# Hybrid transformer layer: the pool branch product computed between projections and attention, the values projected as rows

## The chip, the cores and the metric

The kernel runs on one core of a Trainium2 chip. The metric is the device time of one execution in microseconds, the median of several runs. The engines named below are PE (TensorE, the matmuls), ACT (ScalarE), DVE (VectorE), POOL (GpSimd) and SP, whose queue here only issues DMAs. All data is fp32; a matmul that needs full precision is made of three passes over operands split into a high part (rounded, "hi") and a low part (the rest, "lo"): hi times hi, hi times lo, lo times hi.

## What is computed

One layer for 256 context tokens and 1024 latent tokens, 1280 in all, of width 1024. Cut to what matters here:

```
h = RMSNorm(x) * (1 + scale1) + shift1
q, k, v, xp, ga, gb = split(h @ w_in)            # 1024, 256, 256, 512, 1024, 1024 columns
q, k = rope(RMSNorm(q)), rope(RMSNorm(k))        # 8 query heads, 2 key/value heads of 128
attn = softmax(q k^T / sqrt(128)) v              # latent queries: 1024 latent + 512 cached keys; context queries: 256 context keys
pool = multiscale_pool(xp, w_pool) * pool_scale  # 512 channels
merged = sigmoid(ga) * (attn @ w_branch_a) + sigmoid(gb) * (pool @ w_branch_b)
x = x + gate1 * (merged @ w_out)
# then a second norm, the router, 16 experts and the final norm; k and v of the context tokens are outputs too
```

## The kernel before

Activations are held transposed: 128 channels on the partitions, the 1280 tokens along the free axis, in column groups of 512, 512 and 256 (`GROUPS`). Each engine has its own hand-written instruction list per block; semaphores alone tie them together, and every engine works strictly in the order of its list.

**Block 1, projections.** `project(n, j)` (L311) makes 128 output channels: 8 slices k of 128 input channels, for each the three hi/lo passes over the three column groups, 72 matmuls, into the PSUM half `par_sets[j]`. ACT casts each weight half to `w_hi[j]` once the previous product that used the buffer is finished (`split`, L448), POOL subtracts to get `w_lo[j]` (L539). The pairs come in the order pool input, gates, q, k (`K0` = 14), v (`V0` = 15). The norm and rope of head j of a pair hang on the next product: `sums` (sums of squares by a matmul with ones, L387) as a hook after its slice 2, `spread` (the reciprocal roots to all partitions, L396) after slice 5; between them ACT takes the root and DVE refines it; after them ACT copies the spread rows out, DVE scales the product (L715, frees the PSUM half), makes the sine part (L722), POOL the cosine part (L557), DVE adds (L725). For keys, ACT then casts to `kT_hi` (L518) and POOL makes `kT_lo` (L560). POOL's list in this place reads: w_lo of v half 0, cosine of key head 0, w_lo of v half 1, cosine of key head 1, kT_lo of both heads. The values are projected like everything else (`project(V0, 0)`, `project(V0, 1)`), copied out by ACT (L525), turned into rows by 20 PE transposes (L417), and copied into `vals` by ACT (L530) and DVE (L744). At the end POOL makes the low part of the cached keys (L562). The pool branch's 512 channels go to memory as `poolT`, the sigmoids of the 16 gate rows as `gates`. The block ends in a barrier, the clearing of its semaphores (L749) and a second barrier.

**Block 2, attention.** 16 latent units (one key/value head, 128 tokens, 4 query heads each) and 4 short context units run through `over_units` (L815). `head` makes the scores of one query head (9 matmuls of 512 columns, L875 to L877; DVE finds the maxima, L1022; ACT takes the exponential, L946), `block_` turns the probabilities (L901) and multiplies by values (L885). In front of the steady loop stands an opening of five steps g, in which the four query heads of unit 0 and the four short units are worked side by side: on PE `head(g)`, `short_turn(g-1)` (L926), `short_score(g)` (12 matmuls of 256 columns, L915 to L917), `short_value(g-1)` (L934), the last step with head 0 of unit 1. A short unit's scores go to DVE (maximum L1040, scaled L1041), ACT (four exponentials L965), DVE (normalised, L1047), PE (turned), ACT and DVE (copied out, L970, L1051), PE (values). ACT's and DVE's lists hold the same steps in the same order. POOL splits q (L987, L990) and clears `stage` (L1011) first of all; SP fills the 12 tiles of `y_sum` from it.

**Block 3, merge.** For each of 8 output chunks, `branches` (L1116) makes `attn @ w_branch_a` (8 slices, 72 matmuls) into one PSUM half and `pool @ w_branch_b` (4 slices, 36 matmuls) into the other, all in `product` (L1102). ACT and DVE split the attention output (L1166, L1240) and the pool rows (L1169, L1243) first. DVE multiplies each product by its gate (L1250, L1254) and adds (L1256). Then `merged` is split again (L1185, L1262) and multiplied by `w_out`. Between block 3 and the router block there is one barrier and no clearing.

## Time and profile before

| | us |
|---|---|
| median of 3 runs (lowest, highest) | 1819.08 (1817.8, 1820.91) |
| the profiled execution, its own time | 1816.4 |
| its span in the trace | 1814.5 |
| PE busy | 1616.6 (89%) |
| DVE, ACT, POOL busy | 898.6, 593.2, 393.8 |
| mean granted PE clock, share of full speed | 0.953 |

Some 1.9 us of the execution's time lie outside the span. Times in the trace count from the span's start. In a row of the timeline stand the start, the duration, the engine, the line and operation, what was written and read, how many instructions are merged in the row, and in brackets the idle time before it with the instruction that ended it. A matmul's duration includes its way through the array; back-to-back matmuls start closer together than they last. Block 1 ends at about 597.7 us, block 2 runs from 599.0 to 1028.7, block 3 to 1341.8.

### The profile page before, as it was taken

The numbers are of one execution on the slowest core, as the hardware profiler recorded it, in microseconds if no ns is written. First come the engines' busy times: TensorE is split into PE (matmuls) and PEld (weight loads), VectorE is DVE, ScalarE is ACT, GpSimd is POOL, SyncE is SP. The second block draws the span as 40 slices with busy tenths as digits, with TensorE's granted clock in tenths as the row PEclk, the third lists the DMA queues.
The fourth block names the chain that finished last, engine by engine and source line by source line (L and its number), as shares of the span: only waits on it lengthen the run. The fifth ranks groups of instructions, "written<-read, shape, count | busy, mean of one in ns | idle before, by whom it ended". The sixth has DMA issues, their size and how long they took to land. (4 is left out here: it accounts for less than half of the span.)

```text
span 1814.5 us, 22464 instructions
## 1 busy us (share of the span) xinstructions
PE 1616.6 (89%) x8410; PEld 1278.2 (70%) x8410; DVE 898.6 (50%) x1257; ACT 593.2 (33%) x764; POOL 393.8 (22%) x252
## 2 busy tenths in 40 slices
PE   4899999999999699999999899989977399999950
PEld 4688888878887466666666588878866288888840
DVE  5560000006565666676666543341147667666638
ACT  5211121232222444444444500021123055555513
POOL 1011111112223400000000121121116234445420
PEclk8999999999999899999999999999998599999985
DMA  8133434230100500000000133213032179898945
GB/s 350 67 115 135 159 132 143 109 119 23 46 23 9 200 1 0 0 1 1 0 0 0 58 139 121 85 53 124 23 114 105 65 233 295 266 290 277 281 77 218
DMA packets 38016, 202.28 MB, mean 111 GB/s; under 512 B 4304, under 2 KB 5072, under 8 KB 27728
## 3 DMA queue, kind: packets, MB, share of 16 engines
q1 hardware_dynamic: 28752, 168.07, 24.0%
q0 software_dynamic: 9216, 33.56, 8.3%
q8 instruction: 31, 0.51, 0.1%
q14 instruction: 17, 0.14, 0.0%
HBM read 154.43 MB, written 47.19 MB: 111 GB/s over the span
## 5 line engine op out<-in xcount | busy, mean ns | idle before, releaser
L324 PE MATMUL psum<-h_hi,w_hi 128*128 128x512 f32 (+1 forms) x768 | 199.3, 368 | 7.3 <-DVE h_lo L624 5.5
L324 PE MATMUL psum<-h_lo,w_hi 128*128 128x512 f32 (+1 forms) x768 | 193.6, 361 | 0.0
L324 PE MATMUL psum<-h_hi,w_lo 128*128 128x512 f32 (+1 forms) x768 | 192.5, 359 | 0.0
L885 PE MATMUL psum<-probT,vals 128*128 128x512 f32 x384 | 190.9, 593 | 0.0
L946 ACT ACTIVATE prob<-psum,nmax 128x1536 f32<-128x1536 f32 x64 | 98.6, 1541 | 209.5 <-DVE nmax L1025 209.5
L324 PEld LDWEIGHTS psum<-h_hi,w_hi 128*128 128x128 f32 x768 | 128.7, 190 | 34.7 <-issue 14.3
L539 POOL TENSOR_TENSOR w_lo<-w_raw,w_hi 128x1024 fp32r<-128x1024 f32 x32 | 77.0, 2408 | 348.2 <-ACT w_hi L451 348.2
L901 PEld LDWEIGHTS psum<-ident,prob 128*128 128x128 f32 x768 | 93.0, 141 | 78.6 <-issue 72.7
L324 PEld LDWEIGHTS psum<-h_lo,w_hi 128*128 128x128 f32 x768 | 128.8, 190 | 23.1
L324 PEld LDWEIGHTS psum<-h_hi,w_lo 128*128 128x128 f32 x768 | 128.5, 189 | 23.1
L1022 DVE TENSOR_REDUCE rmax<-psum 128x1 f32<-128x512 f32 x192 | 128.9, 688 | 31.1 <-PE psum L877 30.8
L901 PE MATMUL psum<-ident,prob 128*128 128x128 f32 x768 | 110.7, 274 | 7.9 <-PE psum L885 7.9
L875 PE MATMUL psum<-kT_hi,q_hi 128*128 128x512 f32 x192 | 96.7, 504 | 10.1 <-POOL q_lo L990 8.7
L591 DVE COPY ada_rows<-psum 128x256 f32<-128x256 f32 x24 | 10.2, 425 | 159.7 <-PE psum L279 159.4
L853 DVE COPY probT<-psum 128x512 f32<-128x512 f32 x64 | 44.3, 691 | 85.3 <-PE psum L901 85.3
L1645 POOL DMA_INDIRECT y_sum<-yst,y_row x32 | 74.9, 2340 | 26.0 <-POOL y_row L1643 26.0
L877 PE MATMUL psum<-kT_hi,q_lo 128*128 128x512 f32 x192 | 76.1, 396 | 0.0
L853 ACT COPY probT<-psum 128x512 f32<-128x512 f32 x128 | 70.0, 586 | 18.0 <-PE psum L901 18.0
L876 PE MATMUL psum<-kT_lo,q_hi 128*128 128x512 f32 x192 | 75.3, 392 | 0.0
L885 PEld LDWEIGHTS psum<-probT,vals 128*128 128x128 f32 x384 | 61.6, 190 | 17.4 <-issue 16.1
L1817 DVE TENSOR_TENSOR gu_lo<-gu_raw,gu_hi 128x3072 fp32r<-128x3072 f32 x15 | 50.4, 3358 | 47.5 <-ACT gu_hi L1760 47.5
L987 POOL CAST q_hi<-qT 128x512 fp32r (+1 forms) x16 | 9.7, 609 | 295.4 <-PE psum L877 295.4
(326 smaller groups left out, 3026.3 us busy)
## 6 DMA issues: line engine op xcount, KB each, us to landing
gu_raw<-in_w_gu SPq DMA_DIRECT2D x16, 2048.0 KB, 9.4
ada<-in_w_ada SPq DMA_DIRECT2D x20, 1024.0 KB, 4.8
w_raw<-in_w_in SPq DMA_DIRECT2D x16, 1024.0 KB, 4.8
dn_raw<-in_w_dn SPq DMA_DIRECT2D x16, 1024.0 KB, 6.9
gates<-gst SPq DMA_DIRECT2D x16, 640.0 KB, 3.0
wm_raw<-in_w_merge SPq DMA_DIRECT2D x4, 1536.0 KB, 7.8
y_sum<-stage SPq DMA_DIRECT2D x12, 512.0 KB, 11.9
xt<-in_x SPq DMA_DIRECT2D x10, 512.0 KB, 8.0
```

The costliest lines, as they stand in the source:

```text
L324: mm = pe.matmul(psum[:, par_sets[j] + g:par_sets[j] + g + w], a[j][:, k, :], b[:, k, g:g + w], start=(k == 0 and a is w_hi and b is h_hi) ...
L539: nc.gpsimd.tensor_tensor(w_lo[j][:], w_raw[:, :, j * P:(j + 1) * P], w_hi[j][:], ALU.subtract).then_inc(s[f"w_lo{j}"], 1)
L853: copy(probT[b][g % 2][:], psum[:, TP + 512 * b:TP + 512 * b + 512]).then_inc(s[f"a_t_out{b}"], 1)
L875: pe.matmul(o, q_hi[x.par][:, g, :], kT_hi[:, x.kv, k], start=True, stop=False)
L876: pe.matmul(o, q_hi[x.par][:, g, :], kT_lo[:, x.kv, k], start=False, stop=False)
L877: pe.matmul(o, q_lo[x.par][:, g, :], kT_hi[:, x.kv, k], start=False, stop=True).then_inc(s["a_scored"], 1)
L885: mm = pe.matmul(psum[:, PV + 512 * x.par:PV + 512 * x.par + 512], vals[:, x.key0 // P + c, x.kv * HD:(x.kv + 1) * HD], probT[b][g % 2][:] ...
L901: mm = pe.transpose(psum[:, o:o + P], prob[x.par][:, h, c * P:(c + 1) * P], ident[:])
L946: nc.scalar.activation(prob[x.par][:, g, 0:x.keys], psum[:, SC:SC + x.keys], ACT.Exp, bias=nmax[:, x.par, g:g + 1], scale=SCALE, accum_out ...
L1022: ins = nc.vector.reduce_max(rmax[:, b:b + 1], psum[:, SC + 512 * b:SC + 512 * (b + 1)], AX.X)
L1645: nc.gpsimd.indirect_dma_start(io["y_sum"], bass.IndirectOffsetOnAxis(y_row[j][:], 0), yst[j][:], None, compute_op=ALU.add).then_inc(s[f"e ...
L1817: tt(gu_lo[q][:, 0:GU_FIRST, :], gu_raw[q][:, 0:GU_FIRST, :], gu_hi[q][:, 0:GU_FIRST, :], ALU.subtract).then_inc(s[f"e_gu_lo{q}"], 1)
```

## The change

**Values as rows.** The value weights of both halves lie in one buffer (`v_hi`, `v_lo`). `v_tile(t)` makes the values of 128 tokens at once, with the tokens' `h` as the stationary operand and 256 weight columns moving: 24 matmuls, ten such tiles, 240 matmuls of 256 columns instead of 144 of 512 and 256. They wait for both halves of the value weights; `sums` and `spread` of key head 1 stand after tiles 1 and 3. The copy, the 20 transposes and the copies behind them go; ACT and DVE copy five pairs of tiles into `vals`. The value output is written as rows.

**The pool product.** The 288 matmuls of `pool @ w_branch_b` leave the merge. They become 24 pieces (`fill(f)`: chunk f // 3, column group f % 3, 12 matmuls) placed by the table `FILLS` in the opening of block 2, four to eleven in a step, into two PSUM banks of their own; DVE multiplies each by its gate, and SP writes the rows back over the gates in memory. The casts of the pool rows move to `ready()`, at the end of step 0. PE also ends the opening with a wait for everything in it (`settled`), after head 0 of unit 1. In a step, `short_value` now stands ahead of `short_score`.

**Along with it.** The first split of q for short unit 0 moves from block 2 to the end of POOL's block 1. The clearing of `stage`, and the fill of `y_sum`, move to the middle of attention (`merge_weights`, after unit 8 has begun), where ACT and DVE also make both halves of the first merge weights. In the merge, the chunks' products alternate between the two PSUM halves, and only the finished pool row is added. After block 3 a clearing of semaphores and a barrier are added.

The order of PE's list where the values begin (the end of `project(K0, 1)`, then values); before:

```order
L324 MATMUL psum<-h_hi,w_lo_86 128x512 x2
L324 MATMUL psum<-h_hi,w_lo_86 128x256
L324 MATMUL psum<-h_hi,w_hi_83 128x512 x2
L324 MATMUL psum<-h_hi,w_hi_83 128x256
L324 MATMUL psum<-h_lo,w_hi_83 128x512 x2
```

and after the change:

```order
L323 MATMUL psum<-h_hi,v_lo 128x512 x2
L323 MATMUL psum<-h_hi,v_lo 128x256
L410 MATMUL psum<-v_hi,h_hi 128x256
L411 MATMUL psum<-v_lo,h_hi 128x256
L412 MATMUL psum<-v_hi,h_lo 128x256
```

Before, half 0 of the value weights (`w_hi_83`) follows the last key product (`w_lo_86`, half 1); now the value product, which reads both halves, follows it directly.

ACT's list at the start of attention (exponentials of unit 0's heads `prob`, of the short units `sprob`), before:

```order
L946 ACTIVATE prob_2663,esum<-psum,nmax 128x1536
L965 ACTIVATE sprob,short_sum<-psum,short_nmax 128x256 x4
L946 ACTIVATE prob_2663,esum<-psum,nmax 128x1536
L970 COPY sprobT_2678<-psum 128x512
L965 ACTIVATE sprob,short_sum<-psum,short_nmax 128x256 x4
```

and after the change (`pool_raw` are the pool rows, `wb_raw` the weights of `w_branch_b`):

```order
L1017 ACTIVATE prob_2746,esum<-psum,nmax 128x1536
L1036 ACTIVATE sprob,short_sum<-psum,short_nmax 128x256 x4
L1058 CAST pool_hi_2711<-pool_raw_2719 128x1280
L1058 CAST pool_hi_2712<-pool_raw_2720 128x1280
L1058 CAST pool_hi_2713<-pool_raw_2721 128x1280
L1058 CAST pool_hi_2714<-pool_raw_2722 128x1280
L1053 CAST wb_hi_2729<-wb_raw_2723 128x512
L1053 CAST wb_hi_2730<-wb_raw_2724 128x512
L1017 ACTIVATE prob_2746,esum<-psum,nmax 128x1536
L1041 COPY sprobT_2759<-psum 128x512
```

Six casts stand between step 0's exponentials and step 1's. DVE's list has the six subtractions that belong to them in the same place, ahead of the maxima of head 1.

The diff, cut to its core:

```diff
@@ -124,8 +124,9 @@
+        v_lo = at("v_lo", [P, 2, KC, P], F32R, RW + 16 * KB)
+        w_hi, w_lo = ([v[:, j] for j in range(2)] for v in (v_hi, v_lo))
         stage = at("stage", [P, TOK], F32, RS)
@@ -241,21 +241,20 @@
+                sp.dma_start(io["out_v"].rearrange("(t p) n -> p t n", p=P), vals[:, 0:CTX_TILES, :]).then_inc(s["vout"], 16)
+                sp.wait_ge(s["vout"], 16)
                 for j in range(2):
@@ -402,21 +401,28 @@
                 project(K0, 1, hooks=hooks(4, 0))
-                project(V0, 0, hooks=hooks(4, 1))
-                project(V0, 1)
...
+                def v_tile(t):
+                    o = psum[:, t * KV * HD:(t + 1) * KV * HD]
+                    h = slice(t * P, (t + 1) * P)
+                    for k in range(KC):
+                        pe.matmul(o, h_hi[:, k, h], v_hi[:, :, k, :], start=(k == 0), stop=False)
+                        pe.matmul(o, h_hi[:, k, h], v_lo[:, :, k, :], start=False, stop=False)
+                        mm = pe.matmul(o, h_lo[:, k, h], v_hi[:, :, k, :], start=False, stop=(k == KC - 1))
+                    mm.then_inc(s["v_mm"], 1)
                 for j in range(2):
-                    pe.wait_ge(s["v_raw"], j + 1)
...
-                        mm.then_inc(s["v_ps"], 1)
+                    pe.wait_ge(s[f"w_hi{j}"], V0 + 1)
+                    pe.wait_ge(s[f"w_lo{j}"], V0 + 1)
+                pe.wait_ge(s["ps_free0"], V0)
+                for t in range(TILES):
+                    if t == 6:
+                        pe.wait_ge(s["ps_free1"], V0)
+                    v_tile(t)
+                    if t == 1:
+                        sums(4, 1)
+                    if t == 3:
+                        spread(4, 1)
@@ -516,20 +522,13 @@
+                for p in range(0, HALF, 2):
+                    act.wait_ge(s["v_mm"], 2 * p + 2)
+                    nc.scalar.copy(*v_pair(p)).then_inc(s["v_out_a"], 1)
@@ -555,9 +554,14 @@
                     nc.gpsimd.tensor_tensor(kraw[j][:, CTX:TOK], kraw[j][:, CTX:TOK], cos[:], ALU.mult).then_inc(s["q_cos"], 1)
+                pool.wait_ge(s["q_fin"], HEADS)
                 for j in range(2):
                     pool.wait_ge(s["k_hi"], j + 1)
                     nc.gpsimd.tensor_tensor(kT_lo[:, j, 0:TOK], kraw[j][:], kT_hi[:, j, 0:TOK], ALU.subtract).then_inc(s["k_lo"], 1)
+                pool.wait_ge(s["w_lo1"], N_PAIRS)
+                nc.gpsimd.tensor_copy(sq_hi[:], qT[:, 0:GRP, 0:P]).then_inc(s["sq_first"], 1)
+                pool.wait_ge(s["sq_first"], 1)
+                nc.gpsimd.tensor_tensor(sq_lo[:], qT[:, 0:GRP, 0:P], sq_hi[:], ALU.subtract).then_inc(s["sq_first"], 1)
                 pool.wait_ge(s["cache_hi"], 1)
                 nc.gpsimd.tensor_tensor(kT_lo[:, :, TOK:KEYS], kc_raw[:], kT_hi[:, :, TOK:KEYS], ALU.subtract).then_inc(s["cache_lo"], 1)
@@ -739,31 +743,37 @@
+                dve.wait_ge(s["k_lo"], 2)
+                for p in range(1, HALF, 2):
+                    dve.wait_ge(s["v_mm"], 2 * p + 2)
+                    nc.vector.tensor_copy(*v_pair(p)).then_inc(s["v_out_d"], 1)
@@ -805,8 +815,10 @@
+        FILLS = [((), ()), ((), range(0, 4)), (range(4, 7), range(7, 11)), (range(11, 14), range(14, 18)), (range(18, 21), range(21, 24))]
@@ -820,16 +832,26 @@
+                if g < GRP:
+                    head(units[0], g)
                 if g:
                     short_turn(g - 1)
+                for f in FILLS[g][0]:
+                    fill(f)
+                if g:
+                    short_value(g - 1)
                 if g < GRP:
                     short_score(g)
                     after(units[0], g)
-                if g:
-                    short_value(g - 1)
-                if g < GRP:
                     short_norm(g)
+                else:
+                    pass
+                if g == 0:
+                    ready()
+                for f in FILLS[g][1]:
+                    fill(f)
+            head(units[1], 0)
+            settled()
             for kv in range(KV):
                 with eng.Fori(0, 3) as i:
                     if own:
@@ -855,8 +880,30 @@
+                    load_gb(c)
+                for c in range(KC):
+                    sp.wait_ge(s["g_out"], 3 * (c + 1))
+                    sp.dma_start(io["gates"][KC + c], gbuf[c % 2][:]).then_inc(s[f"g_st{c % 2}"], 16)
+                    if c + 3 < KC:
+                        load_wb(c + 3)
+                    if c + 2 < KC:
@@ -933,7 +980,31 @@
-                over_units(pe, head, block_, lambda x, g: None, tail, short_score=short_score, short_turn=short_turn, short_value=short_value)
+                def fill(f):
+                    c, (g, w) = f // 3, GROUPS[f % 3]
+                    if f == 0:
+                        pe.wait_ge(s["g_pl_hi"], 4)
+                        pe.wait_ge(s["g_pl_lo"], 4)
+                    if f % 3 == 0:
+                        pe.wait_ge(s["g_w_hi"], c + 1)
+                        pe.wait_ge(s["g_w_lo"], c + 1)
+                    if f >= 2:
+                        pe.wait_ge(s["g_out"], f - 1)
+                    for k in range(4):
+                        for w_, b in ((wb_hi, pool_hi), (wb_hi, pool_lo), (wb_lo, pool_hi)):
+                            mm = pe.matmul(psum[:, FILL_PS[f % 2]:FILL_PS[f % 2] + w], w_[c % 3][:, k, :], b[k][:, g:g + w],
+                                           start=(k == 0 and b is pool_hi and w_ is wb_hi), stop=(k == 3 and w_ is wb_lo))
...
+                def settled():
+                    pe.wait_ge(s["c_out_a"], 4)
+                    pe.wait_ge(s["c_out_d"], 4)
+                    pe.wait_ge(s["c_pv_out"], 4)
@@ -974,7 +1045,30 @@
+                def split_wb(c):
+                    act.wait_ge(s[f"g_w_in{c % 3}"], 16 * (c // 3 + 1))
+                    if c >= 3:
+                        act.wait_ge(s["g_mm"], 3 * (c - 2))
+                    nc.scalar.copy(wb_hi[c % 3][:], wb_raw[c % 3][:]).then_inc(s["g_w_hi"], 1)
+                def ready():
+                    act.wait_ge(s["g_pl_in"], 64)
+                    for k in range(4):
+                        nc.scalar.copy(pool_hi[k][:], pool_raw[k][:]).then_inc(s["g_pl_hi"], 1)
+                    for c in range(2):
+                        split_wb(c)
+                def fill(f):
+                    if f % 3 == 0 and f // 3 + 2 < KC:
+                        split_wb(f // 3 + 2)
+                def merge_weights():
+                    act.wait_ge(s["m_wm_in"], 16)
+                    for j in range(2):
+                        nc.scalar.copy(wm_hi[j][:], wm_raw[:, :, j * P:(j + 1) * P]).then_inc(s[f"m_wm_hi{j}"], 1)
+                over_units(act, head, block_, lambda x, g: None, tail, short_score=short_score, short_turn=short_turn, short_value=short_value,
@@ -994,22 +1088,19 @@
+                def merge_weights():
+                    pool.wait_ge(s["g_st0"], 16 * KC // 2)
+                    nc.gpsimd.memset(stage[:, 0:D], 0.0).then_inc(s["a_zero"], 1)
@@ -1049,7 +1140,33 @@
+                def low_wb(c):
+                    dve.wait_ge(s["g_w_hi"], c + 1)
+                    nc.vector.tensor_tensor(wb_lo[c % 3][:], wb_raw[c % 3][:], wb_hi[c % 3][:], ALU.subtract).then_inc(s["g_w_lo"], 1)
+                def ready():
+                    for k in range(4):
+                        dve.wait_ge(s["g_pl_hi"], k + 1)
+                        nc.vector.tensor_tensor(pool_lo[k][:], pool_raw[k][:], pool_hi[k][:], ALU.subtract).then_inc(s["g_pl_lo"], 1)
+                    for c in range(2):
+                        low_wb(c)
+                def fill(f):
+                    c, (g, w) = f // 3, GROUPS[f % 3]
+                    if f % 3 == 0:
+                        dve.wait_ge(s[f"g_gb_in{c % 2}"], 16 * (c // 2 + 1))
+                    dve.wait_ge(s["g_mm"], f + 1)
+                    v = gbuf[c % 2][:, g:g + w]
+                    nc.vector.tensor_tensor(v, v, psum[:, FILL_PS[f % 2]:FILL_PS[f % 2] + w], ALU.mult).then_inc(s["g_out"], 1)
+                    if f % 3 == 0 and c + 2 < KC:
+                        low_wb(c + 2)
+                def merge_weights():
+                    for j in range(2):
+                        dve.wait_ge(s[f"m_wm_hi{j}"], 1)
+                        nc.vector.tensor_tensor(wm_lo[j][:], wm_raw[:, :, j * P:(j + 1) * P], wm_hi[j][:], ALU.subtract).then_inc(s[f"m_wm_lo{j}"], 1)
+                over_units(dve, head, block_, after, lambda x: None, own, 24, short_score, short_norm, short_turn, fill=fill, ready=ready, merge_weights=merge_weights)
@@ -1109,18 +1230,13 @@
-                    pe.wait_ge(s["m_b_out"], 2 * n + j)
-                    product(par_sets[1], wm_hi, wm_lo, j, pool_hi, pool_lo, KC, KM, s["m_mmB"], pool_ready if first else None)
+                    if not isinstance(n, int) or n:
+                        pe.wait_ge(s["m_a_out"], 2 * n + j - 1)
+                    product(par_sets[j], wm_hi, wm_lo, j, h_hi, h_lo, 0, KC, s["m_mmA"], attn_ready if first else None)
                 branches(0, 0, True)
@@ -1238,21 +1348,15 @@
-                for k in range(4):
-                    dve.wait_ge(s["m_pl_hi"], k + 1)
-                    nc.vector.tensor_tensor(pool_lo[:, k, :], pool_raw[:, k, :], pool_hi[:, k, :], ALU.subtract).then_inc(s["m_pl_lo"], 1)
@@ -1270,6 +1374,8 @@
             return dict(x1=x1)
+        nc.clear_and_free_semaphores(early)
```

## Rows read from the trace of the kernel before

**Rows 1.** PE's waits from 584 to 660 us: total, times, longest.
```profile
PE psum L934 <- ACT sprobT L970: 8.8, 4, 3.3
PE psum L875 <- POOL q_lo L990: 8.7, 1, 8.7
```
**Rows 2.** Timeline of PE, end of block 1 to the first score.
```profile
558.77 2.37 PE L387 MATMUL psum<-ones,sq 128*128 128x96 f32 x20
...
584.38 0.74 PE L324 MATMUL psum<-h_hi,w_lo 128*128 128x512 f32 x3
...
602.04 0.80 PE L875 MATMUL psum<-kT_hi,q_hi 128*128 128x512 f32 x1 [8.70 <-POOL q_lo L990]
```
**Rows 3.** Timelines of ACT and POOL in the same stretch.
```profile
553.70 1.24 ACT L494 ACTIVATE sq<-psum 128x1280 f32<-128x1280 f32 x1 [2.21 <-PE psum L324]
...
560.83 2.39 POOL L539 TENSOR_TENSOR w_lo<-w_raw,w_hi 128x1024 fp32r<-128x1024 f32 x1
...
583.72 2.91 POOL L560 TENSOR_TENSOR kT_lo<-kraw,kT_hi 128x1280 fp32r<-128x1280 f32 x1 [2.52 <-ACT kT_hi L518]
595.34 2.34 POOL L562 TENSOR_TENSOR kT_lo<-kc_raw,kT_hi 128x1024 fp32r<-128x1024 f32 x1 [8.72 <-ACT kT_hi L532]
599.04 0.95 POOL L1011 MEMSET stage<- 128x1024 f32 x1 [1.36 <-POOLq L750]
```
**Rows 4.** Stretches: length, busy us (instructions) of PE, PEld, DVE, ACT, POOL; clock, DMA.
```profile
602.00:605.00 3.00, 2.96 (x7) 2.40 (x8) 0.69 (x1) 0.00 (x0) 1.82 (x2) 0.52 1.03 283
...
1048.41:1203.93 155.52, 155.25 (x794) 131.34 (x792) 55.39 (x25) 17.90 (x15) 29.94 (x10) 1.00 0.27 100
```
**Rows 5.** Timelines of PE, ACT and DVE in the opening of attention.
```profile
606.00 0.28 PE L916 MATMUL psum<-kT_lo,sq_hi 128*128 128x256 f32 x1
606.12 0.28 PE L917 MATMUL psum<-kT_hi,sq_lo 128*128 128x256 f32 x1
...
610.92 0.21 ACT L965 ACTIVATION_READ_ACCUMULATOR sprob<-psum,short_nmax 128x1 f32 x1
...
611.38 1.22 DVE L1047 TENSOR_TENSOR sprob<-sprob,short_inv 128x1024 f32<-128x1024 f32 x1
...
617.06 1.95 PE L934 MATMUL psum<-sprobT,vals 128*128 128x512 f32 x4 [1.89 <-ACT sprobT L970]
...
641.94 3.26 PE L934 MATMUL psum<-sprobT,vals 128*128 128x512 f32 x4 [3.31 <-ACT sprobT L970]
645.00 1.90 PE L901 MATMUL psum<-ident,prob 128*128 128x128 f32 x12
```
**Rows 6.** Instructions of the pool rows: count, shortest, median, longest in ns.
```profile
L1169 ACT CAST pool_hi<-pool_raw x4: 1253/1258/1265, 1038.5 to 1042.0; 128x1280 fp32r<-128x1280 f32 x4
L1243 DVE TENSOR_TENSOR pool_lo<-pool_raw,pool_hi x4: 1477/1478/4805, 1044.2 to 1051.8; 128x1280 fp32r<-128x1280 f32 x4
```
**Rows 7.** Groups, opening of attention: busy us, mean ns, idle before.
```profile
L1022 DVE TENSOR_REDUCE rmax<-psum 128x1 f32<-128x512 f32 x15 | 9.6, 681 | 10.6 <-PE psum L877 10.5
...
L946 ACT ACTIVATE prob<-psum,nmax 128x1536 f32<-128x1536 f32 x5 | 7.7, 1540 | 20.1 <-DVE nmax L1025 20.1
```
**Rows 8.** DMAs: count, KB each, us from issue to landing.
```profile
gates<-gst SPq DMA_DIRECT2D x16, 640.0 KB, 3.0
...
pool_raw<-poolT SPq DMA_DIRECT2D x1, 2560.0 KB, 9.5
```
**Rows 9.** Timelines of DVE and PE at a unit's start, middle of attention.
```profile
843.25 0.69 DVE L853 COPY probT<-psum 128x512 f32<-128x512 f32 x1 [3.09 <-PE psum L901]
...
849.06 0.80 PE L875 MATMUL psum<-kT_hi,q_hi 128*128 128x512 f32 x1
```
**Rows 10.** Timelines of PE and DVE: end of the merge, start of the router.
```profile
1209.11 1.41 PE L1102 MATMUL psum<-h_hi,wo_hi 128*128 128x512 f32 x3 [5.19 <-DVE h_lo L1262]
...
1342.14 1.23 DVE L1487 SCALAR_TENSOR_TENSOR h<-x 128x1024 f32<-128x1024 f32 x1 [0.33 <-PEq L1057]
```
**Rows 11.** The page: a group of weight loads, busy us, mean ns, idle before.
```profile
L324 PEld LDWEIGHTS psum<-h_hi,w_hi 128*128 128x128 f32 x768 | 128.7, 190 | 34.7 <-issue 14.3
```

202 lines of the change are left out of this document (92 added, 110 removed).

## Prediction

> **What bounds the kernel now.** The table gives PE 89% busy and no other engine over 50%, so only what shortens PE's work or its breaks can pay, and the views to read are those of its breaks. PE's waits around the end of block 1 come first: four waits of the short units' values on ACT, 8.8 us in all, and one of 8.7 us for POOL's first split of q [rows 1]. The timeline of PE shows where they lie: the last value product issues until 585.1 us, the first score starts at 602.04, and between them stand the value transposes and the block boundary [rows 2]. The timelines of ACT and POOL show what runs meanwhile and, more important, in what order POOL serves value weights and keys [rows 3]. A steady stretch of the merge gives the price of a matmul [rows 4]: 155.5 us from 1048.41 to 1203.93 hold 264 groups of three (columns 512, 512, 256), 0.589 us each, PE without a break.
>
> The change moves matmuls out of a stretch that has no breaks into one that has few. Nothing leaves PE but the 20 transposes. So the question is how much of the breaks is filled, and what new waits come.
>
> **Values.** The product before is 48 groups, 28.3 us. The new one is 240 matmuls of 256 columns; the short scores of that shape start 0.12 us apart [rows 5], which makes 28.4 to 28.8. No difference. But its start moves. It reads both halves of the value weights, and half 1 can be cast only after the last key product, whose end shows as ACT's squaring at 553.70; the low half then waits in POOL's list behind the cosine of key head 0 and is written from 560.83 to 563.2 [rows 3]. Before, value half 0 ran in these 9.7 us; now PE stands. After the 8.7 us break at 602 the granted clock of the next 3 us is 0.52, so about 1.2 GHz instead of 2.4 [rows 4]; I charge 1.4 us for that after each long break. Two tiles (5.7 us) later come the sums of key head 1: 563.3 + 1.4 + 5.7 = 570.4, not 558.77 [rows 2]. The spread follows after sums and two tiles (7.9 us) instead of sums and three slices (7.5). So everything behind key head 1 is 12.0 us late. Its kT_lo ended at 586.6 [rows 3] and will end at 598.6; behind it in POOL's list stand the moved split of short unit 0 (2.05 us, from the q split that fills 602.04 - 599.04 less the clear of 0.95 [rows 2, 3]) and the cached keys' 2.34: 603.0 us, against 597.7. PE ends its tiles near 596, ACT's and DVE's copies are done by 600, SP's cached values are asked for at 598.6 and land some 4 us later: all hidden. The clear of 0.95 is gone from the front of block 2. The first score starts 5.3 - 0.9 = **4.4 us later** than before, although 17 us of gap looked free. Bounds 3.5 and 7, the latter if the DMAs end last.
>
> **The opening of attention** took 43.0 us, 602.04 to 645.00 [rows 5]. Added are 96 groups, 56.5 us. Gone are the 8.8 us on ACT [rows 1], because pieces stand between turning and values, and 1.7 us of half clock at the end, where the matmuls after a wait of 3.31 us took 3.26 and the transposes 1.90 (1.95 and 1.5 elsewhere) [rows 5]. New are:
> - Step 0's casts. ACT's short exponentials end at 611.1 [rows 5]. Four casts of 1.26 [rows 6] and two small ones follow, to 617.1. DVE ends normalising at 612.6, then makes four subtractions of 1.48 and two of 0.6, to 619.7. Only now does it find head 1's maxima, three of 0.68 and 0.4 for the rest, and ACT the exponential of 1.54 and the copy of 0.6 [rows 7]: short_value(0) starts at 624.2. PE had its last work at 613.5 with the turning (the score of step 1 now stands behind the values). Wait 10.7, and 1.4 for the clock. The pool rows' DMA is no part of it: 9.5 us from issue to landing [rows 8] is 608.8.
> - In steps 1 to 3 DVE reaches the pieces after a short unit's maxima, exponentials and normalising, 5.6 us after the score (607.0 to 612.6 in step 0). PE can be two pieces ahead, 5.65 us in step 1, 4.2 in steps 2 and 3, where one is narrow. With the product by the gate that leaves 0.8 + 2.0 + 1.8 = 4.6.
> - Head 0 of unit 1 now stands last, so head 1 of it meets DVE's maxima and ACT's exponential 5.0 us after that head's start, with 3.4 us of PE work between: 1.6.
> - The weights of chunk c+3 are asked for only when chunk c is out, behind a 640 KB store (3.0 us to landing [rows 8]), and ACT and DVE wait for them in their lists. No row shows such a load of 512-byte pieces; between 0 and 10 us in all, I take 1.5, near the store's time.
>
> Sum 43.0 + 56.5 - 8.8 - 1.7 + 10.7 + 1.4 + 4.6 + 1.6 + 1.5 = 108.8, **65.8 more**; bounds 58 (half the first wait, no late weights) and 77.
>
> At the subtractions a rule matters. Of the four before, three took 1.48 us and one, with POOL's w_lo beside it, 4.8 [rows 6]; in the new place POOL's short split is over by 609, so I take 1.48 for all. The Trainium skill, SBUF — State Buffer, section "SBUF: two separate sides", says that DVE with two SBUF inputs and a reading GpSimd lock each other out for a whole instruction. By that rule, the trace agrees, a collision here would add up to 3.3 us and none means the sum as it stands.
>
> **Middle of attention.** ACT's two casts stand where it would copy out turned probabilities; DVE, which idled 3.09 us before 843.25 [rows 9], now waits for them and subtracts twice (1.2 each), to 845.8. Copy 0.7, normalising 1.2, maxima 2.4, exponential 1.6 lead to 851.5 for the head that started at 849.06: **2.4**, bounds 0 and 3. The clear and the fill of y_sum have slack of hundreds of us.
>
> **Merge.** 96 groups less, 56.5, and a wait of 0.3 for the pool rows: **-56.8**, bounds -58 and -56. A chunk is now 14.1 us, while DVE needs three operations of 1.5 and ACT and POOL 4 for the weights: still PE's. The break of 5.19 before w_out [rows 10] stays, since behind the last product stand DVE's multiply, add and split as before; what the last pool product covered, the casts of earlier chunks, ACT does faster (1.26) than PE uses them (1.77). **Last barrier:** with a clearing, 1.36 between blocks [rows 3], without 0.33 [rows 10]: **1.0**, bounds 0 and 1.4.
>
> **Sum.** 4.4 + 65.8 + 2.4 - 56.8 + 1.0 = +16.8 us. The profiled execution took 1816.4, 2.7 below the median, and would take 1833.2; the same on the median 1819.1 is 1835.9. I say 1835. Bounds: 1819 + 3.5 to 1819 + 32.
>
> **Rivals.**
> - *The pieces fill the breaks* (faster). If the casts of step 0 hid under other work, 10.7 + 1.4 would be about 2, and if DVE kept pace, 4.6 and the 1.5 would go: the opening grows by 49.6. With a free value start (4.4 gone, and 5 us off the boundary) the whole is 49.6 - 5 + 2.4 - 56.8 + 1 = -9, 1810. It decides as soon as ACT is done with the casts before 608. For it: 20 us of waits in [rows 1]. Against: ACT's list, in which the six casts stand ahead of head 1's exponential. 0.07.
> - *Even.* The opening's stalls come out at half and the value start costs nothing: +3, 1821. 0.08.
> - *Late weights.* If each of the five later loads holds ACT 3 us longer than thought: +15 more, 1850. 0.12.
> - *Weight loads count.* A load lasts 190 ns [rows 11] and a tile's matmul only 0.12 us. Were loads in the way, 96 more of them are 18 us: 1854. Against: the short scores, each with its load, start 0.12 apart [rows 5]. 0.03. The Trainium skill, TensorE: Matmul & The Clock Gate, sections "LDWEIGHTS (loading the stationary operand)" and "The mechanism", gives 107 ns for 128 columns and lets a load overlap a running matmul only in another row group; by that rule no load would be hidden here, and the trace disagrees.
> - The forecast itself, 1826 to 1846: 0.70.
>
> About 0.2%, 3.6 us, is what a measurement of this kernel can tell from none. Faster 0.07, within 0.08, slower 0.85. The range of 8 in 10 leaves out the first two rivals' lower part and the last: 1823 to 1847.
>
> **What would show it.** PE idle from 553.5 to 563.3 before the first tile, released by POOL's low half; first score near 606.4; one break of 10 us in front of short_value(0) with DVE and ACT in the pool rows; the opening near 109 us; the merge 57 us shorter. If the first piece starts within 5 us of the short turning, or the tiles follow the key product at once, the forecast falls, and towards 1810.

## The result, and the profile after

| | us |
|---|---|
| before, median of 4 runs beside the change (lowest, highest) | 1819.99 (1817.8, 1821.1) |
| after, median of 4 runs (lowest, highest) | 1838.76 (1837.81, 1840.18) |
| ratio after to before, 95% interval | 1.0103 (1.0087 to 1.0119) |
| the profiled execution of after, its span | 1840.18, 1838.4 |

The change makes the kernel 18.8 us slower; 1835, with 1823 to 1847, was predicted. PE is 88% busy (1620.6 us, before 1616.6) and the mean granted clock fell from 0.953 to 0.945.

For the comparison the trace is cut at six places, each the start of an instruction: ACT's squares of key head 1, the first score, the first turning of unit 0's probabilities, the first matmul of the merge, of `w_out`, of the router. The second trace of before is that of the experiment before_again.

| stage, us | before | before, 2nd trace | after | after less before |
|---|---|---|---|---|
| squares to first score | 48.34 | 48.42 | 54.14 | +5.8, +5.7 |
| opening: first score to first turning | 42.96 | 46.37 | 110.72 | +67.8, +64.4 |
| first turning to merge | 386.90 | 386.72 | 390.14 | +3.2, +3.4 |
| merge | 177.21 | 177.20 | 120.43 | -56.8, -56.8 |
| `w_out` to router | 133.03 | 135.88 | 139.46 | +6.4, +3.6 |
| router to end | 472.36 | 472.16 | 470.13 | -2.2, -2.0 |

With the 0.3 us by which the squares came earlier in the trace of after, the stages add up to the 23.9 us between the spans. The first trace of before (1816.4) lies under its median; against the second (1821.64) the spans are 18.7 us apart.

PE's waits of after between 548 and 720 us (total, times, longest):

```profile
PE psum L922 <- POOL q_lo L1084: 10.4, 1, 10.4
PE psum L981 <- ACT sprobT L1041: 10.1, 1, 10.1
PE psum L410 <- POOL v_lo L538: 9.7, 1, 9.7
PE psum L997 <- DVE stage L1161: 4.0, 3, 2.2
PE psum L997 <- DVE gbuf L1161: 2.2, 1, 2.2
```

The 8.8 us of [rows 1] on ACT are gone. In their place stand 10.1 us before the first short values, 6.2 for pieces (4.0 behind DVE's products, `stage`, and 2.2, `gbuf`, where DVE's list stood behind late weights) and 9.7 before the value tiles, and the break at the block boundary grew from 8.7 to 10.4. Timelines of POOL, PE and SP around the value product, answering to [rows 2, 3]:

```profile
558.18 2.34 POOL L556 TENSOR_TENSOR stage<-stage,cos 128x1024 f32<-128x1024 f32 x1 [12.40 <-DVEq L727]
...
560.47 2.34 POOL L538 TENSOR_TENSOR v_lo<-w_raw,v_hi 128x1024 fp32r<-128x1024 f32 x1
...
563.07 0.55 PE L410 MATMUL psum<-v_hi,h_hi 128*128 128x256 f32 x1 [9.72 <-POOL v_lo L538]
...
593.83 0.28 PE L411 MATMUL psum<-v_lo,h_hi 128*128 128x256 f32 x1
...
593.95 0.28 PE L412 MATMUL psum<-v_hi,h_lo 128*128 128x256 f32 x1
...
599.42 0.42 SPq L253 DMA_DIRECT2D out_v<-vals  x1
...
600.80 2.34 POOL L566 TENSOR_TENSOR kT_lo<-kc_raw,kT_hi 128x1024 fp32r<-128x1024 f32 x1
...
605.41 0.61 POOL L1081 CAST q_hi<-qT 128x512 fp32r<-128x512 f32 x1 [2.27 <-POOLq L755]
```

The tiles begin when the low half of value weights 1 is written, which stands behind the cosine. Inside them a matmul starts every 0.12 us, each with its own load of weights, so the loads cost nothing. POOL is done at 603.14, but the boundary then takes 2.27 us, not 1.36: the value output was issued at 599.42 and needed 4.4 us, so it landed near 603.8, behind POOL.

The opening of attention in after, PE and ACT, answering to [rows 5]:

```profile
616.95 4.74 ACT L1058 CAST pool_hi<-pool_raw 128x1280 fp32r<-128x1280 f32 x4
...
618.59 1.09 PE L973 MATMUL psum<-ident,sprob 128*128 128x128 f32 x8 [1.82 <-DVE sprob L1138]
...
627.56 1.54 ACT L1017 ACTIVATE prob<-psum,nmax 128x1536 f32<-128x1536 f32 x1 [4.83 <-DVE nmax L1116]
...
629.81 3.75 PE L981 MATMUL psum<-sprobT,vals 128*128 128x512 f32 x4 [10.12 <-ACT sprobT L1041]
...
641.96 0.38 PE L997 MATMUL psum<-pool_hi,wb_hi 128*128 128x256 f32 x1 [0.70 <-DVE stage L1161]
...
665.83 0.65 PE L997 MATMUL psum<-pool_hi,wb_hi 128*128 128x512 f32 x1 [2.21 <-DVE stage L1161]
...
691.38 0.50 PE L997 MATMUL psum<-pool_hi,wb_hi 128*128 128x512 f32 x1 [1.11 <-DVE stage L1161]
...
698.93 0.47 PE L997 MATMUL psum<-pool_hi,wb_hi 128*128 128x512 f32 x1 [2.23 <-DVE gbuf L1161]
```

The short values take 3.75 us instead of 1.95. The pieces stand four to seven in a step (the table `FILLS`), from step 1 on; the first starts at 635.62. Stretches of the same trace (columns as in [rows 4]): the one behind the 10.1 us wait, a chunk of three pieces, the one around the 2.2 us wait at 665.83, and the one behind that at 698.93:

```profile
629.80:635.60 5.80, 5.79 (x16) 3.73 (x17) 0.00 (x0) 0.59 (x1) 0.00 (x0) 0.53 0.00 0
643.48:650.42 6.94, 6.94 (x37) 5.84 (x36) 2.41 (x5) 0.62 (x1) 0.00 (x0) 1.00 0.68 205
663.50:672.30 8.80, 6.59 (x24) 5.21 (x23) 3.84 (x6) 0.62 (x1) 0.51 (x1) 0.81 0.46 136
698.90:717.10 18.20, 18.17 (x81) 14.64 (x82) 4.45 (x9) 0.59 (x1) 0.00 (x0) 0.91 0.30 115
```

The granted clock is 0.53 for 5.8 us behind the long wait, and 0.81 over the 8.8 us around the short one: about half speed (1.2 GHz, "half clock" from here on) for some 3 us of it. Behind the other wait of 2.2 us, at 698.93, it is 0.91 over 18.2 us.

PE in the middle of attention, at the start of `w_out` and at the router, answering to [rows 9, 10]:

```profile
925.87 0.50 PE L922 MATMUL psum<-kT_hi,q_hi 128*128 128x512 f32 x1 [1.68 <-ACT prob L1017]
...
1228.81 1.40 PE L1223 MATMUL psum<-h_hi,wo_hi 128*128 128x512 f32 x3 [5.22 <-DVE h_lo L1366]
...
1368.27 2.13 PE L1503 MATMUL psum<-ident,m 128*128 128x128 f32 x12 [1.80 <-PEq L1378]
```

The merge weights cost 1.7 us, the break before `w_out` is as it was, and the boundary to the router took 0.89 us before and takes 1.80 now, with its clearing and second barrier.

Last, the place that the prediction left out. DVE and POOL split `merged`, then x is loaded over it. Timelines of DVE, POOL, SP and PE, of before, then of after, and under them the 4 us of after behind PE's wait:

```profile
1207.47 11.22 DVE L1262 TENSOR_TENSOR h_lo<-merged,h_hi 128x1280 fp32r<-128x1280 f32 x6 [0.30 <-DVE merged L1256]
...
1218.85 0.38 SPq L1090 DMA_DIRECT2D x<-in_x  x1
...
1235.10 0.44 PE L1142 MATMUL psum<-ident,stage 128*128 128x128 f32 x2 [1.41 <-DVE x L1270]
```

```profile
1227.17 14.01 DVE L1366 TENSOR_TENSOR h_lo<-merged,h_hi 128x1280 fp32r<-128x1280 f32 x6 [0.30 <-DVE merged L1360]
...
1228.44 3.01 POOL L1339 TENSOR_TENSOR h_lo<-merged,h_hi 128x1280 fp32r<-128x1280 f32 x1 [23.41 <-ACT h_hi L1296]
1233.09 3.94 POOL L1339 TENSOR_TENSOR h_lo<-merged,h_hi 128x1280 fp32r<-128x1280 f32 x1 [1.63 <-ACT h_hi L1296]
...
1241.33 0.39 SPq L1211 DMA_DIRECT2D x<-in_x  x1
...
1257.92 0.69 PE L1258 MATMUL psum<-ident,stage 128*128 128x128 f32 x2 [4.25 <-DVE x L1374]
```

```profile
1257.90:1261.90 4.00, 3.98 (x12) 3.40 (x13) 0.99 (x2) 1.04 (x1) 1.44 (x1) 0.50 0.09 39
```

DVE's six subtractions take 14.0 us instead of 11.2. In both kernels ACT casts `merged` only after the last attention product. Before, the last pool product came behind that one: POOL's first slice was made at 1201.76, while DVE had none to make, and only POOL's second met DVE's six. Now the attention product is the last one, both of POOL's slices fall among DVE's six, and the load of x, which waits for all eight, is asked for 12.5 us after the first matmul of `w_out` instead of 9.7. That is 2.8 us later: PE waits 4.25 us instead of 1.41, and 4 us at clock 0.50 follow.

### The profile page after: what moved, and what is told of

Read it like the earlier page. It is cut to its first block and busy times, and to the rows that moved or that the text cites. A ratio compares the mean times of both kernels' runs of the same rounds, so it can differ in the third digit from the quotient of the medians.

```text
span 1838.4 us, 22677 instructions
## 1 busy us (share of the span) xinstructions
PE 1620.6 (88%) x8486; PEld 1286.2 (70%) x8486; DVE 893.2 (49%) x1282; ACT 592.9 (32%) x771; POOL 377.8 (21%) x249
## 5 line engine op out<-in xcount | busy, mean ns | idle before, releaser
L323 PE MATMUL psum<-h_hi,v_hi 128*128 128x512 f32 x720 | 187.1, 368 | 7.3 <-DVE h_lo L628 5.5
L323 PE MATMUL psum<-h_lo,v_hi 128*128 128x512 f32 x720 | 181.6, 361 | 0.0
L323 PE MATMUL psum<-h_hi,v_lo 128*128 128x512 f32 x720 | 180.4, 359 | 0.0
L538 POOL TENSOR_TENSOR v_lo<-w_raw,v_hi 128x1024 fp32r<-128x1024 f32 x32 | 77.0, 2408 | 347.8 <-ACT v_hi L457 347.8
L323 PEld LDWEIGHTS psum<-h_hi,v_hi 128*128 128x128 f32 x720 | 120.7, 190 | 33.4 <-issue 14.3
L323 PEld LDWEIGHTS psum<-h_lo,v_hi 128*128 128x128 f32 x720 | 120.8, 190 | 21.7
L323 PEld LDWEIGHTS psum<-h_hi,v_lo 128*128 128x128 f32 x720 | 120.4, 189 | 21.6
L922 PE MATMUL psum<-kT_hi,q_hi 128*128 128x512 f32 x192 | 95.3, 497 | 15.0 <-POOL q_lo L1084 10.4
L878 ACT COPY probT<-psum 128x512 f32<-128x512 f32 x128 | 69.9, 588 | 16.6 <-PE psum L948 16.6
```

The source lines that it names most:

```text
L323: mm = pe.matmul(psum[:, par_sets[j] + g:par_sets[j] + g + w], a[j][:, k, :], b[:, k, g:g + w], start=(k == 0 and a is w_hi and b is h_hi) ...
L538: nc.gpsimd.tensor_tensor(w_lo[j][:], w_raw[:, :, j * P:(j + 1) * P], w_hi[j][:], ALU.subtract).then_inc(s[f"w_lo{j}"], 1)
L878: copy(probT[b][g % 2][:], psum[:, TP + 512 * b:TP + 512 * b + 512]).then_inc(s[f"a_t_out{b}"], 1)
L922: pe.matmul(o, q_hi[x.par][:, g, :], kT_hi[:, x.kv, k], start=True, stop=False)
```

## The experiments

Twelve runs. Each expectation was written before its run. "Change" is the kernel after. "Stage" lengths are those of the table above, measured in the one trace of each run. Each ratio is to the kernel before on the same chip, with its 95% interval.

**values_alone.** The value hunks of the diff in the kernel before, nothing of the pool product.

> The kernel before with the value part of the change alone: values as rows, the split of short unit 0 moved into block 1, the row output; pool product in the merge as before. Theory: the value part costs what the trace of the change shows up to the first score, 5.5 us, and 0.95 more, since POOL's clearing of `stage` still stands ahead of its first split here: first score near 608.5 instead of 602.0, nothing else moves, 1820.0 + 6.4 = 1826.4 (1825 to 1828). The pool part of the change would then be worth the other 12.4. Rival, the value part is hidden in the gap of 17 us before attention: within 2 us of 1820, and all of the loss is the pool part's. Rival, its 240 loads of weights slow the product itself: the ten tiles take over 30 us where 28.4 is their matmul time.

1823.86 us, 1.0024 (1.0015 to 1.0034). Squares to first score 54.72 us, 6.4 more, as expected; opening 42.91 and merge 177.22, unchanged. The time is 2.5 below the expectation; in its trace the stretch from router to end takes 470.2 us, 2.1 less than before's, while `w_out` (135.85) is like before's second trace. So the value part costs some 4 us (2.7 to 6.2), and the pool part, by difference, the other 14 or 15.

**low_first.**

```diff
-                for j in range(2):
-                    split(V0, j)
+                split(V0, 0)
+                split(V0, 1)
+                for j in range(2):
                     pool.wait_ge(s["q_sin"], HEADS + j + 1)
```

> The change with one swap in POOL's list: the low half of value weights 1 ahead of the cosine of key head 0. Theory: the 9.7 us wait at 553.5 is the place in POOL's list and nothing else; the cast it needs is done at 555.6 and POOL is idle to 558.2, so the first tile starts at 558.1 instead of 563.1, the cosine is not delayed (it waits for DVE's sine until 558.2), and all behind moves 5.0 us earlier: first score 602.5, time 1838.8 - 5.0 = 1833.8. Rival, a transfer (cached values, value output) or the cached keys set the end of block 1: the tiles start 5 us earlier but the first score by less than 2 us, 1837 to 1839.

1835.18 us, 1.0088 (1.0072 to 1.0105), 3.6 less. The cause is confirmed, the size is not (1833.8 was expected): POOL starts at once, but its subtraction takes 3.37 us instead of 2.34, since DVE's sine products run beside it.

```profile
554.28 3.37 POOL L538 TENSOR_TENSOR v_lo<-w_raw,v_hi 128x1024 fp32r<-128x1024 f32 x1 [9.84 <-ACT v_hi L457]
557.91 0.55 PE L410 MATMUL psum<-v_hi,h_hi 128*128 128x256 f32 x1 [5.91 <-POOL v_lo L538]
```

Tiles 3.8 us earlier, first score 4.0 (50.10 instead of 54.14).

**sums_first.** With `low_first`:

```diff
+                sums(4, 1)
                 for j in range(2):
                     pe.wait_ge(s[f"w_hi{j}"], V0 + 1)
...
                     if t == 1:
-                        sums(4, 1)
-                    if t == 3:
                         spread(4, 1)
```

> The change with the swap in POOL's list of `low_first`, and on PE `sums` of key head 1 ahead of the first tile (it needs only the squares) and `spread` after tile 1 instead of tile 3. Theory: in the change, the chain of key head 1 hangs on PE's order of tiles; freed of it, it ends 8 us earlier and the tiles themselves set the end of block 1. From ACT's squares of key head 1 to the first score: 54.1 us in the change, 50.1 with the swap alone, about 44.5 here, which is less than the 48.3 of the kernel before; time 1838.8 - 9.6 = 1829.2 (1828 to 1831). Rival, the transfers that end the block (cached values, value output) come after the tiles anyway: 47 to 49 us, 1832 to 1834.

1826.17 us, 1.0032 (1.0021 to 1.0044), 3 us better than expected. Squares to first score 42.29 us: 11.9 less than the change, 7.8 less than `low_first`, 6.1 less than before. So the order of PE's list, not a transfer, set how late block 1 ends; the transfer adds only what it adds to the boundary, which takes 2.27 us here as in the change. The opening, which these edits don't touch, is 1.8 us shorter too (108.97): PE's busy time in it is 1.5 us less.

**casts_behind.** `ready()` moves from the end of step 0 to step 1, behind `short_turn(0)`.

> The change with the casts and subtractions of the pool rows (`ready`) moved on ACT and DVE from the end of step 0 to behind head 1's exponential and the first copies of step 1. Theory: the 10.1 us wait before the first short values is their place in the two lists. It becomes 3.4 us (618.6 turning, 620.8 maxima, 622.5 exponential, 623.1 copy), and the rest of the casts is met again in front of the first piece, which can start at about 630.2 instead of 635.6: the opening is 5 us shorter, and up to 1 us of half clock goes, 1833.5 (1832 to 1835). Rival, only the sum of ACT's and DVE's work counts and the wait reappears whole in front of the first piece: 1838 to 1839. Rival, the landing of the pool rows holds it: no change either, and the casts themselves would show waits for a transfer.

1834.68 us, 1.0090 (1.0073 to 1.0107). PE:

```profile
620.21 3.75 PE L981 MATMUL psum<-sprobT,vals 128*128 128x512 f32 x4 [3.31 <-ACT sprobT L1041]
628.11 0.47 PE L997 MATMUL psum<-pool_hi,wb_hi 128*128 128x512 f32 x1 [1.95 <-DVE wb_lo L1146]
```

The wait of 10.1 becomes 3.3 and 2.0; the first piece starts 23.4 us after the first score instead of 28.1. The place in ACT's and DVE's lists was the cause. The opening is only 3.7 us shorter (107.06): the short values behind the wait of 3.3 us still take 3.75, and PE's busy time in the opening is 1.6 us more than in the change (92.7 against 91.1), half clock again.

**opening_early_casts.** The casts in three parts, the subtractions on POOL (only POOL's part of the edit is shown).

```diff
+                def ready(n):
+                    for k in {1: (0, 1), 3: (2, 3)}.get(n, ()):
+                        pool.wait_ge(s["g_pl_hi"], k + 1)
+                        nc.gpsimd.tensor_tensor(pool_lo[k][:], pool_raw[k][:], pool_hi[k][:], ALU.subtract).then_inc(s["g_pl_lo"], 1)
```

> The change with the casts of the pool rows spread over ACT's idle time (two ahead of head 0's exponential, two after the first short exponentials, the weights' casts after the copy of step 1) and the four subtractions on POOL, which idles there, instead of DVE. Theory: nothing stands ahead of head 1's maxima and exponential any more, so the first short values start 4.5 us after their turning instead of 11.2, the first piece about 7 us after it instead of 17.0, and less half clock follows: opening 100 to 102 us instead of 110.7, time 1838.8 - 9.5 = 1829.3 (1827 to 1832). Rival, POOL's subtractions and DVE's operations lock each other out and the stall moves to another place: opening above 106, 1834 or more.

1832.34 us, 1.0060 (1.0043 to 1.0077), opening 103.54. The first short values start 4.4 us after their turning; but the turning itself is 1.4 us later than in the change, because the table of the exponential (1.28 us) is now loaded between the casts and head 0's exponential, and one of DVE's small operations stretched to 2.06 us beside POOL. Partly as expected: the opening is 7.2 us shorter, where 9 to 11 were expected.

**pieces_mended.**

```diff
+                    for f in FILLS[g][1][:ahead]:
+                        fill(f)
                     short_norm(g)
...
-                    if f % 3 == 0 and c + 2 < KC:
+                    if f % 3 == 2 and c + 2 < KC:
                         low_wb(c + 2)
```

`ahead` is 1 on DVE and 0 elsewhere; ACT's casts of the weights move like `low_wb`.

> The change with two edits in the lists of ACT and DVE: the split of the weights of chunk c+2 stands behind the last piece of chunk c instead of its first, and in steps 1 to 3 DVE takes the first piece ahead of the short unit's normalising. Theory: the four waits of PE for pieces are of two kinds, 0.7 + 2.2 + 1.1 us behind the normalising and 2.2 us behind weights whose load landed at 696.8. Both go (together under 0.8 us left), and the half clock of 1.6 us after the 2.2 us wait with them: opening 105 to 106 us instead of 110.7, time 1838.8 - 5.3 = 1833.5 (1832 to 1835). Rival, DVE is simply full there: each wait moves to a neighbour, 1837 to 1839. If only the wait of the weights goes, 1836.5.

1828.90 us, 1.0047 (1.0030 to 1.0063): 9.9 less where 5.3 were expected. No wait for a piece is left. The whole opening of the change, then of this kernel, and a stretch inside it:

```profile
607.52:718.24 110.72, 91.13 (x430) 73.25 (x431) 54.40 (x86) 27.69 (x60) 9.92 (x10) 0.89 0.39 131
```

```profile
606.75:707.24 100.49, 87.15 (x429) 70.99 (x430) 54.91 (x86) 27.37 (x60) 9.94 (x10) 0.91 0.44 145
640.00:700.00 60.00, 60.00 (x317) 49.86 (x316) 31.11 (x52) 13.01 (x31) 6.15 (x6) 1.00 0.52 165
```

6.2 us of waits went, and PE's busy time for the same work fell by 4.0: that was half clock, for the most part behind the waits (their two stretches above cost 3.3). Which of the two edits gave how much was not run.

**merged_dve.** DVE makes all eight low halves of `merged`, POOL none.

> The change with all eight low halves of `merged` made by DVE, where POOL made two of them (slices 3 and 7). Theory: in the trace of the change two of DVE's subtractions take 4.2 us beside POOL's two, where one did before, so the load of x, which waits for all of them, is asked for 2.8 us later, PE waits 4.25 instead of 1.41 us before the first transposed chunk, and its clock is at half for some us behind that. Without POOL DVE needs 8 x 1.48 = 11.8 instead of 14.0: the wait becomes 2.0, the clock cost of 2.4 falls to 0 to 1.5, 1838.8 - 2.2 - 1.5 = 1835.1 (1834 to 1837). Rival, the load of x is late for another reason (traffic, its own length of 15.5 us): the wait stays above 4, 1838 to 1839.

1835.54 us, 1.0091 (1.0073 to 1.0108).

```profile
L1358 DVE TENSOR_TENSOR h_lo<-merged,h_hi x8: 1482/1483/1493, 1225.6 to 1235.4; 128x1280 fp32r<-128x1280 f32 x8
```

Eight subtractions, none above 1.49 us, 11.3 us in all. The load of x is asked for 9.7 us after the first matmul of `w_out`, as before:

```profile
1236.94 0.39 SPq L1207 DMA_DIRECT2D x<-in_x  x1
```

PE's wait for x is 2.44 us, `w_out` to router 135.61 instead of 139.46. DVE does more and is done sooner: the stretched operations were the collision.

**x_in_pieces.** The load of x in ten transfers, tile t as soon as the slices of `merged` under it are split.

> The change with the load of x for the last addition cut into ten transfers, each asked for as soon as the slices of `merged` whose place it takes are split. Theory: PE's wait of 4.25 us before the first transposed chunk of w_out is the load of x, asked for only when the last of eight slices is split; the half clock behind it comes from the wait. Cut up, the last of it lands 8 us before it is needed: wait 0.5, from the first matmul of w_out to the router 133 us instead of 139.5 (135.6 with DVE alone on the slices), time 1838.8 - 6 = 1832.8 (1831.5 to 1834.5). Rival, ten transfers are slower than one or crowd the splits: over 136 us, 1835 or more.

1832.25 us, 1.0068 (1.0051 to 1.0085). Wait 0.48 us, `w_out` to router 133.29: as expected. The load, not the splits themselves, is what PE waited for.

**before_x_in_pieces.** The same edit in the kernel before.

> The kernel before with the load of x in ten transfers and nothing else. Theory: in the one trace of before PE waits 1.41 us for x, of which 0.9 can go; but the load alone took 15.1 to 16.4 us in six traces, and a wait of 2.7 us in another kernel with the same end of the merge was followed by half clock for 4 us. The median should therefore gain more than the trace shows: 1819.5 - 1 to - 3, 1816.5 to 1818.5, and the stage from w_out to the router take 132.3 us. Rival, no gain within 0.1%: then the part of 6 us that this edit gave in the change was owed to the change alone.

1815.08 us, 0.9977 (0.9967 to 0.9987). `w_out` to router 132.07; 4.1 us below the median of before, a little more than the 1 to 3 expected. It is more than the 0.9 us of wait that the first trace of before showed could go, though the trace explains only part of it: from router to end it takes 469.5 us against 472.4 and 472.2. That part is open.

**before_again.**

> The kernel before, unchanged, for a second trace of it. Theory: the first trace (1816.4 us) lies under the median of 1819 since the load of x landed early in it (wait 1.41 us, no half clock); stage by stage the change's trace is then compared with a lucky one. This trace should show the stages up to w_out within 0.5 us of the first (squares to first score 48.3, opening 43.0, merge 177.2) and w_out to the router anywhere from 133 to 136 us. Rival, the stages before w_out vary too (by over 1 us): then the stage-by-stage differences of the change's trace are no better than that.

1821.53 us, 0.9999 (0.9990 to 1.0009). Squares to first score and merge repeat within 0.1 us. The opening does not (46.37 against 42.96): the rival holds there. The whole opening in the first trace, then in this one:

```profile
602.04:645.00 42.96, 30.95 (x142) 22.00 (x143) 31.71 (x53) 19.21 (x49) 17.92 (x14) 0.94 0.44 169
```

```profile
601.37:647.74 46.37, 35.38 (x141) 25.18 (x142) 31.79 (x53) 19.34 (x49) 17.44 (x14) 0.83 0.41 159
```

PE's busy time for the same work is 4.4 us more, at a mean clock of 0.83 instead of 0.94; the waits for other engines are no longer in sum (11.0 us against 12.0). So the clock makes the difference. In the traces of values_alone and before_x_in_pieces the same opening took 42.91 and 43.00. The first 4 us of attention ran at clock 0.64 in the first trace and 0.50 in this one, the next 4 at 1.00 and 0.74. The load of x took 16.6 us against 15.2, the wait was 2.83 against 1.41, and the stage 135.88.

**all_mended** and **values_x_mended.** The first is the change with these mends together, save that POOL keeps its two slices of `merged`, and with two new ones (POOL splits the merge weights, the table of the exponential is loaded early). The second is the kernel before with the mended value part and the load in pieces, the pool product left in the merge.

> The change with all mends together: POOL's low half of value weights 1 first, `sums` and `spread` of key head 1 early, the casts of the pool rows spread and their subtractions on POOL, pieces and weights reordered on DVE and ACT, the load of x in ten transfers; besides, both merge weights split by POOL in the middle of attention, and a first tiny exponential on ACT so that the table of the exponential is loaded before the casts. Theory: the mends act at different places, so they add: stage lengths as measured one by one, 11.9 + 10.2 + 7.2 + 1.1 + 6.1 + 1.7 = 38 us off the change, less what two mends of the opening share (1 to 3): 1802 to 1806, some 0.9% faster than the kernel before. Rival, the opening keeps a stall of another kind (POOL's four subtractions lock DVE once the pieces start sooner): 1808 to 1812. If it is no faster than the kernel with values and x mended alone, moving the pool product has no worth by itself.

> The kernel before with the value part alone, mended (POOL's swap, `sums` and `spread` early), and the load of x in ten transfers; the pool product stays in the merge. Theory: from ACT's squares of key head 1 to the first score 43.3 us (42.3 as measured with the mends, and 0.95 for POOL's clearing) instead of 48.3; w_out to router 132 to 133 us; opening 43.0 and merge 177.2 as before. 1819.5 - 5.0 - 1 to 2.8 for x = 1812 to 1814. Rival, the load in pieces gives nothing here since the wait for x was only 1.4 us: 1815.

all_mended: 1807.17 us, 0.9928 (0.9915 to 0.9941). values_x_mended: 1808.50 us, 0.9933 (0.9919 to 0.9946). Both beat both kernels; the intervals overlap, so they can't be told apart. all_mended is 1.2 us above the range expected for it, values_x_mended 3.5 us below its own. The stages of all_mended: 42.23, 95.20, 388.17, 120.40, 135.44. The opening is 1.9 us longer than the 93.3 which the gains of opening_early_casts and pieces_mended leave, with 5.5 us of waits around the first short values; `w_out` is 2 us longer than in x_in_pieces; the wait there is the same 5.22 us, but half clock lasts longer behind it (below). The stages of values_x_mended: 42.98, 45.67, 386.40, 177.19, 132.09. So moving the pool product, with these mends, is worth nothing that can be measured. In the two traces it shortens opening and merge together by 7.3 us (215.6 against 222.9, of which 2.9 are a slower clock in the opening of values_x_mended, 0.87 against 0.94 in before), and gives back 1.8 in the middle of attention and 3.4 from `w_out` to the router, 0.9 of them the added clearing.

## Why the prediction was right, and where it was wrong

| term | predicted | measured |
|---|---|---|
| wait before the tiles; load of weights in them | 9.7; none | 9.72; none |
| end of kT_lo, of POOL's list | 598.6, 603.0 | 598.94, 603.14 |
| first score (from the squares) | +4.4 (3.5 to 7) | +5.8 |
| pieces | +56.5 | +55.5 (8 x 6.94) |
| ACT's waits gone | -8.8 | -8.8 |
| wait before the first short values | 10.7 | 10.1 |
| waits of pieces behind normalising | 4.6 | 4.0 |
| late weights | 1.5 | 2.2 |
| head 1 of unit 1 | 1.6 | 1.5 |
| clock in the opening | -0.3 (-1.7 + 1.4) | about +4.4 |
| middle (merge weights) | +2.4 | +1.7 |
| merge | -56.8 | -56.8 |
| barrier and clearing | +1.0 | +0.9 |
| `w_out` | 0 | +5.5 (+2.7 to the second trace) |

*Right.* The sign, the cause and nearly every place: slower because the 96 groups went from a stretch without breaks into one whose breaks are made by ACT's and DVE's lists. The order of the lists decided (casts_behind for ACT and DVE, low_first for POOL, sums_first for PE), and the merge gave back what it should. The first piece started 17 us after the short turning, so the rival that fills the breaks fell, and "even" with it. The rival of late weights fell too: 2.2 us in all, in one wait. The rival of the weight loads fell by the 240 matmuls 0.12 us apart. The Trainium skill, TensorE: Matmul & The Clock Gate, section "The mechanism", says that a load overlaps running matmuls only when the row group differs; by that sentence every load would have been charged, and the traces disagree.

*First score, 1.4 short.* "All hidden" was wrong for the DMAs: SP's value output landed last, near 603.8, behind POOL's 603.1. The upper bound of the term named this case ("if the DMAs end last"). The boundary's 2.27 us show it: 0.9 of the 1.4. The other 0.5 is the clock again: the two tiles behind the 9.7 us wait took 7.5 us (563.07 to 570.61), where 1.4 + 5.7 were summed.

*The clock, the term that failed in the opening.* Only the long wait was charged, with 1.4. Behind the 10.1 us wait clock 0.53 over 5.8 us cost 2.7 to 2.9, and the two waits of 2.2 us, charged with nothing, cost some 1.6 each (8.8 x 0.19, 18.2 x 0.09); less the 1.7 that goes, that makes about +4.4. pieces_mended shows the price by itself: 6.2 us of waits carried some 4.0 us of slow matmuls.

*`w_out`, the term that was missing.* The sentence "what the last pool product covered, the casts of earlier chunks, ACT does faster (1.26) than PE uses them (1.77)" is true for PE: its break before `w_out` is 5.22 as before. But it stopped at PE. Behind the same splits stands the load of x, and POOL's slices now collide with DVE's. The prediction had [rows 6] in hand, with 4.8 us for a subtraction beside POOL's; it asked about a collision at the place to which the subtractions moved, not at the place from which the cover was taken. merged_dve shows the cause: six in 14.0 us with POOL beside, eight in 11.3 without. It and x_in_pieces take back 3.9 and 6.2 of the 6.4 us. The Trainium skill, SBUF — State Buffer, section "SBUF: two separate sides", says that a DVE operation with two SBUF inputs and a GpSimd operation that reads SBUF hold a shared pair of ports for a whole instruction each, the later one waiting; the traces agree.

The predicted sum was +16.8, the measured one +18.8 by the medians (15.8 to 21.7 by the ratio's interval). It came that near partly by luck: stage by stage against the first trace of before the terms miss 9.6 us (clock, `w_out`, transfers). Two came back between the router and the end, unexplained (values_alone and before_x_in_pieces have them too), and five are the difference between the two traces of before, most of it clock.

Two slips in the working change nothing: [rows 1] hold 17.5 us of waits, not 20, and +3 on 1819 is 1822, not 1821.

## What to carry to other kernels

Work moved under other work is covered only if the lists that feed it have their operations in the right order; here three edits of order were worth 4 us (a subtraction before a cosine), 8 (sums before tiles) and 10 (products with the gate before a normalising, together with weights split later), and the move itself nothing. When a product is taken away, ask what ran beside it on every engine, and follow those operations past PE to the transfers that wait for them. Price a break of PE with the half clock behind it, and look at a second trace before one stage is read to the microsecond.

## What was not expected of the hardware

A break does not have one price. Behind the same 5.22 us wait before `w_out`, three stretches of 4 us, in x_in_pieces and in all_mended:

```profile
1227.56:1231.56 4.00, 3.54 (x9) 2.54 (x9) 4.00 (x2) 4.00 (x4) 2.64 (x1) 0.57 0.40 131
1231.56:1235.56 4.00, 3.86 (x20) 3.32 (x21) 4.00 (x2) 0.29 (x2) 3.73 (x1) 1.00 0.61 196
1235.56:1239.56 4.00, 3.94 (x21) 3.12 (x20) 4.00 (x3) 0.00 (x0) 0.21 (x1) 1.00 0.94 356
```

```profile
1200.38:1204.38 4.00, 3.54 (x9) 2.55 (x9) 4.00 (x2) 4.00 (x4) 2.65 (x1) 0.50 0.39 131
1204.38:1208.38 4.00, 3.86 (x11) 3.22 (x12) 4.00 (x2) 0.29 (x2) 3.73 (x1) 0.50 0.63 197
1208.38:1212.38 4.00, 4.00 (x19) 3.37 (x18) 4.00 (x3) 0.00 (x0) 0.17 (x1) 0.81 1.01 380
```

PE did the same before it in both: 20 us without a break at clock 1.00. In one the clock is back at 2.4 GHz within 4 us, in the other it stays at 1.2 GHz beyond 8, and the first wait for x comes 2.1 us later (27.47 us after the first matmul of `w_out` instead of 25.34). The Trainium skill, TensorE: Matmul & The Clock Gate, section "What's actually happening", says that the number of slow matmuls varies from run to run; the traces agree. Here it moved a stage by 2.1 us (`w_out`) and by 3.4 (the opening of before).

A DVE and a POOL operation that meet can cost either side: POOL's 2.34 us subtraction took 3.37 beside DVE's sine (low_first), DVE's 1.48 us subtraction took 4.2 beside POOL's (before and after). And one transfer of 5 MB took from 15.1 to 16.6 us over the traces, enough to turn a wait of 1.4 us with full clock behind it into one of 2.8 with half.
